# Differential attention in a two-layer trunk: scores through three PSUM pairs in turn, the turned map and the values through the fourth

## The reference

```python
s = jnp.einsum('bqhcd,bkhcd->bhcqk', qblk, k).astype(jnp.float32) * scale    # dh = 64, c = 2 maps
pr = jax.nn.softmax(s, axis=-1)
a = (pr[:, :, 0] - lam * pr[:, :, 1]).astype(v.dtype)
return jnp.einsum('bhqk,bkhe->bqhe', a, v)                                   # e = 128
```

## Time and profile before

| | |
|---|---|
| median of three runs | 1902.31 us |
| the profiled execution | 1897.74 us, of which the span of its instructions 1895.8 |
| mean granted clock of TensorE | 0.927 of full speed |
| busy: TensorE, weight load | 1531.4 us (81%), 708.3 |
| busy: VectorE, ScalarE, GpSimd | 592.7 us (31%), 245.6, 229.3 |
| the attention loop (282 to 372 us of the span) | 90 us |

### The profile page before, as it was taken

The page is one execution under the profiler, slowest core; times in us unless marked ns, Lnnn a source line. Parts: engine busy times, 40 slices in busy tenths (PEclk is TensorE's granted clock), DMA queues, the critical chain, the costliest instruction groups (busy, mean ns, idle before and its releaser), DMA issues.

```text
span 1895.8 us, 18497 instructions
## 1 busy us (share of the span) xinstructions
PE 1531.4 (81%) x6500; PEld 708.3 (37%) x6500; DVE 592.7 (31%) x1124; ACT 245.6 (13%) x489; POOL 229.3 (12%) x354
## 2 busy tenths in 40 slices
PE   4999897698699777778778589999499887887882
PEld 2445445445333323223333334545433332333330
DVE  2499447633422111111112331123512111111114
ACT  2111025511000000000000311001100000000001
POOL 0024020000111111111111001000011111111110
PEclk9999998898799999999999789999689999999986
DMA  9753512015699999999997745220989999999995
GB/s 341 246 178 134 182 52 88 23 60 201 260 419 419 421 420 420 421 420 420 420 419 305 294 171 192 82 111 34 352 344 419 420 420 420 420 421 420 420 388 194
DMA packets 117028, 559.09 MB, mean 295 GB/s; under 512 B 13981, under 2 KB 14806, under 8 KB 63466
## 3 DMA queue, kind: packets, MB, share of 16 engines
q1 hardware_dynamic: 96224, 518.64, 68.0%
q0 software_dynamic: 11392, 21.08, 2.9%
q10 hardware_dynamic: 9354, 18.58, 2.8%
HBM read 546.63 MB, written 26.28 MB: 302 GB/s over the span
## 4 chain that ended last, share of the span: by engine, by line
PE 40%; DMA 24%; SPq 8%; issue 4%; DVE 4%; ACT 2%; ACTq 0%; DVEq 0%; POOLq 0%; POOL 0%
PE psum_pair_B L1582 15%; DMA weight_ring<-w_up 13%; DMA scratch<-w_up 9%; SPq L465 7%; PE psum_pair_C L1600 5%; PE psum_pair_B L1496 4%; PE psum_pair_C L1528 4%; PE psum_pair_D L1528 4%; PE psum_pair_A L1496 3%; PE psum_pair_D L1518 1%; DMA weight_ring<-w_ada 1%; PE psum_pair_C L1437 1%; PE psum_pair_D L1589 1%; DVE scratch L1186 1%; DMA scratch<-expert_rows 1%
## 5 line engine op out<-in xcount | busy, mean ns | idle before, releaser
L1582 PE MATMUL psum_pair_B<-weight_ring,gates_by_token 128*64 128x512 f32 x1472 | 350.9, 631 | 77.2 <-DMA weight_ring<-w_up 57.1
L1582 PEld LDWEIGHTS psum_pair_B<-weight_ring,gates_by_token 128*64 128x64 f32 x1472 | 127.6, 145 | 296.1 <-issue 293.4
L1186 DVE TENSOR_TENSOR scratch<-psum_pair_B,scratch 128x256 f32<-128x256 f32 x68 | 28.9, 425 | 622.0 <-ACT scratch L789 622.0
L1582 PE MATMUL psum_pair_B<-scratch,gates_by_token 128*64 128x512 f32 x704 | 173.9, 650 | 41.0 <-DMA scratch<-w_up 31.6
L1600 PE MATMUL psum_pair_C<-weight_ring,scratch 128*64 128x512 f32 x736 | 169.2, 600 | 26.1 <-issue 23.7
L611 POOL DMA_INDIRECT expert_rows<-scratch,scatter_rows x68 | 69.7, 1025 | 817.4 <-DVE scratch L1198 790.9
L1496 PE MATMUL psum_pair_A<-scratch,weight_ring 128*128 128x128 f32 (+1 forms) x512 | 146.7, 445 | 4.4 <-DVE scratch L1236 2.8
L1496 PE MATMUL psum_pair_B<-scratch,weight_ring 128*128 128x128 f32 (+1 forms) x512 | 142.2, 436 | 0.0
L789 ACT ACTIVATE scratch<-psum_pair_B 128x256 f32<-128x256 f32 x68 | 26.1, 384 | 890.8 <-PE psum_pair_B L1582 890.8
L1279 DVE SCALAR_TENSOR_TENSOR weight_ring<-weight_ring,params 128x655 f32<-128x655 f32 x120 | 117.0, 975 | 5.0 <-DVE gates_by_token L993 1.0
L1582 PEld LDWEIGHTS psum_pair_B<-scratch,gates_by_token 128*64 128x64 f32 x704 | 60.1, 150 | 152.4 <-issue 152.4
(11 more groups left out here) (308 smaller groups left out, 1418.4 us busy)
## 6 DMA issues: line engine op xcount, KB each, us to landing
weight_ring<-w_gate SPq DMA_DIRECT2D x46, 2048.0 KB, 33.6
weight_ring<-w_up SPq DMA_DIRECT2D x46, 2048.0 KB, 34.7
weight_ring<-w_down SPq DMA_DIRECT2D x46, 2048.0 KB, 34.4
weight_ring<-w_ada SPq DMA_DIRECT2D x24, 2048.0 KB, 8.6
scratch<-w_up SPq DMA_DIRECT2D x22, 2048.0 KB, 34.6
scratch<-w_down SPq DMA_DIRECT2D x22, 2048.0 KB, 34.7
scratch<-w_gate SPq DMA_DIRECT2D x22, 2048.0 KB, 33.4
weight_ring<-w_in_e SPq DMA_DIRECT2D x5, 2048.0 KB, 13.0
```

The source lines that it names most:

```text
L1186: tt(HID[par], PB[B_][:, 512 * par + 256:512 * par + 512], SIL[par], ALU.mult).then_inc(sig("hidden", l), 1)
L1582: ins = mm(PB[B_][CAP * q:CAP * (q + 1), 512 * par:512 * par + 512].rearrange("p (u n) -> p u n", u=2), XGT[par][:, at:at + CAP], w[:, :, ...
```

## The change

Scores are made one map at a time. The 40 maps, counted through all units, go through pairs A, B and C in turn, and TensorE makes four of them in step 0 and two in each further step, so that it works on the maps of unit i+1 in step i. The turned map and the values share pair D: the turned map has columns 0 to 639, the values columns 768 to 895. On TensorE the values of unit i-2 now stand ahead of the turn of unit i-1; on VectorE the maxima of unit i now stand ahead of `mixed` of unit i-1. Nothing is computed differently.

```diff
-        for i in range(NU + 2):
-            if i < NU:
-                put(A_, "s", i, 0), put(B_, "s", i, 1)
-            if 1 <= i <= NU:
-                put(C_, "aT", i - 1)
+        for m in range(2 * NU):
+            put(m % 3, "s", m // 2, m % 2)
+        for i in range(NU + 2):
             if i >= 2:
                 put(D_, "av", i - 2)
+            if 1 <= i <= NU:
+                put(D_, "aT", i - 1)
...
-                took(ts(OR[:, t, h * 128:(h + 1) * 128], p[:, 0:128], sr[:, u % 2, 0:1], None, ALU.mult), "av", u)
+                took(ts(OR[:, t, h * 128:(h + 1) * 128], p[:, 768:896], sr[:, u % 2, 0:1], None, ALU.mult), "av", u)
...
             for i in range(NU + 2):
+                if i < NU:
+                    maxima(i)
                 if 1 <= i <= NU:
                     mixed(i - 1)
-                if i < NU:
-                    maxima(i)
                 if i >= 2:
                     heads_out(i - 2)
...
-            def scores(u):
+            def scores(u, c):
                 t, h = UNITS[u]
-                ps = [fill(pe, "s", u, c) for c in range(2)]
-                rows = [slice(DH * c, DH * (c + 1)) for c in range(2)]
-                q = [qT[rows[c], h, t * 128:(t + 1) * 128] for c in range(2)]
+                p = fill(pe, "s", u, c)
+                rows = slice(DH * c, DH * (c + 1))
+                q = qT[rows, h, t * 128:(t + 1) * 128]
                 if t < 4:
-                    for c in range(2):
-                        mm(ps[c][:, 0:NS], q[c], kT[rows[c], h, 0:NS], start=True, stop=True)
-                    for c in range(2):
-                        filled(mm(ps[c][:, NS:NS + PAST], q[c], kcT[rows[c], h, :], start=True, stop=True), "s", u, c)
+                    mm(p[:, 0:NS], q, kT[rows, h, 0:NS], start=True, stop=True)
+                    filled(mm(p[:, NS:NS + PAST], q, kcT[rows, h, :], start=True, stop=True), "s", u, c)
                 else:
-                    for c in range(2):
-                        filled(mm(ps[c][:, 0:NP], q[c], kT[rows[c], h, NS:], start=True, stop=True), "s", u, c)
+                    filled(mm(p[:, 0:NP], q, kT[rows, h, NS:], start=True, stop=True), "s", u, c)
...
-                    ins = mm(p[:, 0:128], AT[:, u % 2, i * 128:(i + 1) * 128], v, start=(i == 0), stop=(i == len(vs) - 1))
+                    ins = mm(p[:, 768:896], AT[:, u % 2, i * 128:(i + 1) * 128], v, start=(i == 0), stop=(i == len(vs) - 1))
...
             for i in range(NU + 2):
-                if i < NU:
-                    scores(i)
+                for m in ((0, 1, 2, 3) if i == 0 else (2 * i + 2, 2 * i + 3)):
+                    if m < 2 * NU:
+                        scores(m // 2, m % 2)
+                if i >= 2:
+                    values(i - 2)
                 if 1 <= i <= NU:
                     turn(i - 1)
-                if i >= 2:
-                    values(i - 2)
```

## The result

The changed kernel took 1953.24 us (median of four executions: 1952.30, 1954.19, 1958.50 and 1924.49) against 1901.18 before. The forecast was 1918, in a range of 1911 to 1928. The first comparison gave a ratio of 1.0206 (1.016 to 1.0251), which counts only two of the four executions, 1952.30 and 1924.49, as the other two were taken for disturbed. A second measurement of the same kernel gave 1957.38 and a ratio of 1.0311 (1.0296 to 1.0326), with all its executions between 1953 and 1960. So there are two kinds of execution: nearly all near 1955, one near the forecast.

The account below looks back on a forecast made before the run. An order of waits, not a full engine, was taken to pace the attention loop. Start -3.6, twelve periods +17.2 and end +2.0 gave +15.6 us, so 1902.31 + 15.6 = 1918 us, range 1911 to 1928.

Parts of the forecast that it names:

- The ring through pair D: Attention loop: turn waits for heads_out, closing a cycle of waits through three in-order queues; 5.78 us a unit against 4.41.
- Q: head_squares on ScalarE, standing ahead of the next exp in the ring: 0.42 us with its accumulator read and following step.
- V: Values product on TensorE, in the ring after the second map: 1.32 us from its start to heads_out.
- H: heads_out on VectorE, taking the values from pair D: 0.35 us, plus 0.14 to TensorE, so 0.49.
- E: Exp of one map on ScalarE, in the ring: 0.88 us with its read, then 0.15 to TensorE.
- The start: Loop start to first heads_out: 13.4 us against 17.0, so -3.6, assuming full clock with a pause of 1.3.
- rival B: Slower start: the clock falls in the shorter pause too, costing 4 to 7 us more, 1922 to 1925 us; chance 0.20.
- twelve periods: Attention loop from first to thirteenth heads_out: 5.78 us each, 69.4 against 52.2, so +17.2.
- half clock throughout: Rival for the whole attention loop: TensorE at half clock, some 9 us a period, 1963 us in all; chance 0.05.
- The end: Loop after the thirteenth heads_out, with the prompt's four short units: 22.6 us against 20.6, so +2.0.
- the loss passes on whole: After the loop: the next expert page and the weight stream start later by the full +15.6 us.
- Rival A: Faster: wait on heads_out does not decide, loop runs at TensorE's own 3.98 us a unit, 1893 us; chance 0.06.

Follow-up runs that it names:

- filler_half: Changed kernel plus one unused 128 x 512 product per full-size unit ahead of its first map, on rows 0 to 63 only: 1924.99 us, ratio 1.0134.
- squares_later: Changed kernel with head_squares moved on ScalarE to between the two exps of a later unit: 1925.18 us, ratio 1.0137.
- before_split: Kernel before the change, with each full-size unit's second map started only when its first is done: 1913.54 us, ratio 1.0067.
- v_first_nudge: Changed kernel with the values product between the two maps, plus one small 128 x 128 product per full-size unit: 1906.19 us, ratio 1.0042.
- after_nudge: Changed kernel plus one 128 x 128 product on 64 rows per full-size unit, ahead of its first map: 1955.44 us.
- the fillers: Two kernels: the changed one plus one unused 128 x 512 product per full-size unit, on all 128 rows or on 64: 1921.93 and 1924.99 us.
- after_nudge2: Changed kernel plus two 128 x 128 products on 64 rows per full-size unit, ahead of its first map: 1923.74 us, ratio 1.0124.
- v_first: Changed kernel with the values product of unit i-2 between the two maps of unit i+1 on TensorE: 1948.66 us.

## Why the prediction was wrong

- The ring through pair D was right, in its order and in its size: 5.78 forecast, 5.72 in three kernels that differ from the change by hidden work alone, and 5.43 without Q. That the size came so near has some luck in it: in filler_half the map takes 1.27 until V starts (1.15 forecast) and V 1.42 until H (1.32), while Q takes 0.29 (0.42) and E with the step to TensorE 0.93 (1.03). That VectorE would wait about 2 us for the values was right (2.24).
- The start was right in the first profile alone, and by luck: first heads_out at 295.77 (295.5 forecast), clock 1.00. Its pause was 2.28 us, not 1.3 (row of 286.96 below), because the first two maps went through together. In the ten other profiles of kernels that make their maps one at a time in this start, the clock fell between 287 and 292 us, so the fall that rival B described, given 0.20, is what mostly happens there.
- The step that failed is the clock behind the start. The prediction priced all twelve periods at full clock, and gave the half clock throughout 0.05, because "at half clock TensorE would work nearly without a gap, and after such a stretch the clock came back before". It is what happened: with TensorE 95% busy and nearly no gap the clock stayed at 0.50, and a period took 8.56. At full clock the loop did not hold either. Its pauses there were shorter than the 1.1 of before, 0.44 and 0.58 us a unit (rows below, in brackets, from the last unit before the clock fell), and the busy share was higher. The rows of before showed a hold and a return with both halves of the array at work, and were carried over to a loop without that; but that the single maps are the cause is not shown, as filler_half, squares_later and before_split held 1.00 with single maps.

```profile
286.96 1.12 PE L1722 MATMUL psum_pair_A<-scratch 64*128 64x512 f32 x2 [2.28 <-ACT scratch L891]
...
296.18 0.77 PE L1731 MATMUL psum_pair_D<-square_consts,scratch 128*128 128x128 f32 x5 [0.44 <-DVE scratch L1339]
...
298.80 1.54 PE L1722 MATMUL psum_pair_A<-scratch 64*128 64x512 f32 x2 [0.58 <-ACT scratch L891]
```

- The price of this rival was 1963 us, with 9.0 a period; measured 8.56 and 1952 to 1959. Its three TensorE terms were sized well (6.4 forecast; 1.36 + 2.43 + 2.54 = 6.33 in the unit shown above); the steps of the other engines take 2.23 there, where the sum had some 2.6.
- In numbers: the loop ran from 282.29 to 426.56, 144.3 us, where the forecast had 105.4 (13.4 + 69.4 + 22.6). Of the 38.9 missing, 30.9 lie in the twelve periods (295.77 to 396.06, 100.3 against 69.4), 7.9 behind them. The end was priced at full clock too: even in filler_half it took 28.7 against 22.6, at 0.50 from 372 us on. Its start, where the clock fell, took 15.2 (283.36 to 298.60) against 13.4. So even the kernels whose periods ran at full clock took 1922 to 1925 us, not 1918.
- That the loss passes on whole was right (54.6 of 54.6).
- Rival A was priced too well: with single maps TensorE itself needs more than the 3.98 taken. In v_first_nudge, where it never pauses, a unit takes 4.78, of which the small product takes 0.33 (324.31 to 324.64), so some 4.45 is left, an estimate from these rows:

```profile
324.31 0.48 PE L1723 MATMUL psum_pair_C<-scratch 64*128 64x128 f32 x2
324.64 1.02 PE L1725 MATMUL psum_pair_C<-scratch 64*128 64x512 f32 x2
```

What stays open: why the half-clock loop stays there although TensorE is busy nearly or quite throughout, and why it ended within a few us in four kernels with a little more work for TensorE, but not in after_nudge. Single maps, pauses and the period were each tried; none alone accounts for all the runs. What the runs do show is the price: with the same ring, the clock at 0.50 costs 2.84 us a unit (8.56 against 5.72 in the fillers and after_nudge2).

## What to carry to other kernels

When two users share a buffer in turn, follow the in-order queues of all engines around once: a wait between two engines often closes a ring, and its sum is the new period. A time taken from rows at full clock is worth only what the clock is; where a change makes TensorE's work thinner (one half of the array for two), price the stage at both clocks, and don't take the profile's busy share as a sign that the clock holds. If it does not, a few cheap products in a pause can be worth more than any waiting they cause: here two small ones a unit took the time from about 1955 to 1924 us.

## What the runs showed of the hardware

- TensorE can be 100% busy by the profile for 110 us at a granted clock of 0.50 (v_first), and 100% busy at 1.00 with a small product more (v_first_nudge).
- Maps on the two halves of the array run together without alternate issue, if both are free to start: in the changed kernel's first step they start 0.01 us apart, though in the kernel's text all of one stands ahead of the other.

```profile
282.29 0.66 PE L1722 MATMUL psum_pair_A<-scratch 64*128 64x512 f32 x1 [0.45 <-ACT scratch L866]
...
282.30 0.69 PE L1722 MATMUL psum_pair_B<-scratch 64*128 64x512 f32 x1
```

- One kernel has two times, 1924 us (mean granted clock 0.922) and 1952 to 1960 us (0.894 to 0.903). The execution of 1924 was not profiled.
